# Zero-padded full-height score matmuls in a two-layer hybrid attention backbone

## The reference

```python
def _diff_attn(q, k, v, lam):
    s = jnp.einsum('bqhid,bkhid->bhiqk', q, k, preferred_element_type=jnp.float32)
    p = jax.nn.softmax(s * (ATTN_HEAD_DIM ** -0.5), axis=-1)
    a = p[:, :, 0] - lam * p[:, :, 1]
    return jnp.einsum('bhqk,bkhe->bqhe', a.astype(v.dtype), v)
```

## Time and profile before

| | |
|---|---|
| median of 3 runs | 1786.41 us (1783.9 to 1787.53) |
| profiled execution: time | 1787.53 us |
| profiled execution: span from first to last instruction | 1785.6 us |
| busy: TensorE, VectorE, ScalarE, GpSimd | 1716.1, 1084.9, 609.5, 76.4 us |
| mean granted clock of TensorE | 0.984 |
| attention, layer 0 | 557 to 602 us |
| attention, layer 1 | 1524 to 1553 us |

### The profile page before, as it was taken

One profiled execution on the slowest core, in us unless ns is written; L12 is line 12 of the kernel. 1 busy time (PEld: TensorE's weight loads), 2 busy tenths in 40 slices (PEclk: granted clock), 3 DMA queues, 4 the chain that ended last, 5 costly groups with the idle time before them and its releaser, 6 DMA issues.

```text
span 1785.6 us, 25611 instructions
## 1 busy us (share of the span) xinstructions
PE 1716.1 (96%) x8952; PEld 1446.0 (81%) x8952; DVE 1084.9 (61%) x1666; ACT 609.5 (34%) x905; POOL 76.4 (4%) x140
## 2 busy tenths in 40 slices
PE   3999999999998999999999999999999999799999
PEld 1888888887785678888888878888888878589999
DVE  2877777235678667777762377777523277665544
ACT  2322222124534643222221242222222263544443
POOL 0000000000001000000000000000000000000000
PEclk9999999999999999999999999999999999899999
DMA  9355555332241125555552225555333224035554
GB/s 362 130 187 177 176 178 175 106 95 71 91 134 48 36 71 177 177 176 177 175 177 94 95 83 189 176 178 183 109 96 104 84 85 149 28 130 180 185 179 151
DMA packets 69684, 248.62 MB, mean 139 GB/s; under 512 B 7424, under 2 KB 8448, under 8 KB 69504
## 3 DMA queue, kind: packets, MB, share of 16 engines
q1 hardware_dynamic: 51200, 180.79, 31.3%
q0 software_dynamic: 18432, 67.12, 11.6%
HBM read 246.83 MB, written 1.05 MB: 139 GB/s over the span
## 4 chain that ended last, share of the span: by engine, by line
PE 90%; DVE 5%; ACT 2%; SPq 1%; issue 1%; DMA 1%; DVEq 0%; ACTq 0%
PE ps L973 28%; PE ps L975 28%; PE ps L974 28%; PE ps L1025 3%; DMA raw<-wstream 1%; DVE shared_b L683 1%; DVE wlo L582 1%; DVE nmax L871 1%; PE ps L1191 1%; PE ps L1164 1%; DVE xl L669 1%; SPq L270 1%; ACT prob L484 1%; PE ps L1112 0%; SPq L266 0%
## 5 line engine op out<-in xcount | busy, mean ns | idle before, releaser
L582 DVE TENSOR_TENSOR wlo<-raw,whi 128x1024 fp32r<-128x1024 f32 x320 | 392.1, 1225 | 603.5 <-ACT whi L330 602.8
L973 PE MATMUL ps<-xh,whi 128*128 128x512 f32 (+1 forms) x1880 | 683.0, 363 | 23.1 <-DVE xl L669 18.3
L330 ACT ACTIVATE whi<-raw 128x1024 fp32r<-128x1024 f32 x320 | 339.1, 1060 | 1064.3 <-PE ps L975 1047.6
L975 PE MATMUL ps<-xh,wlo 128*128 128x512 f32 (+1 forms) x1880 | 665.2, 354 | 0.0
L974 PE MATMUL ps<-xl,whi 128*128 128x512 f32 (+1 forms) x1880 | 665.0, 354 | 0.0
L973 PEld LDWEIGHTS ps<-xh,whi 128*128 128x128 f32 x1880 | 361.3, 192 | 81.3 <-issue 25.3
L974 PEld LDWEIGHTS ps<-xl,whi 128*128 128x128 f32 x1880 | 362.9, 193 | 49.3 <-issue 3.8
L975 PEld LDWEIGHTS ps<-xh,wlo 128*128 128x128 f32 x1880 | 362.3, 193 | 47.8
L604 DVE SCALAR_TENSOR_TENSOR shared_a<-wm,cs,shared_a 128x512 f32<-128x512 f32 x448 | 307.6, 747 | 0.0
L973 PE MATMUL ps<-ah,whi 128*128 (+2 forms) x704 | 255.5, 363 | 0.0
L975 PE MATMUL ps<-ah,wlo 128*128 (+2 forms) x704 | 255.2, 363 | 0.0
(11 more groups left out here) (101 smaller groups left out, 842.1 us busy)
## 6 DMA issues: line engine op xcount, KB each, us to landing
raw<-wstream SPq DMA_DIRECT2D x320, 512.0 KB, 3.4
wm<-wmod POOLq DMA_DIRECT2D x128, 512.0 KB, 3.6
wm<-wmod SPq DMA_DIRECT2D x3, 2048.0 KB, 21.8
h<-x_t SPq DMA_DIRECT2D x1, 2048.0 KB, 12.7
wm<-wmod SPq DMA_DIRECT2D x2, 1024.0 KB, 20.7
K<-cols SPq DMA_DIRECT2D x1, 1163.0 KB, 14.4
out_t<-h SPq DMA_DIRECT2D x8, 128.0 KB, 2.5
K<-cols SPq DMA_DIRECT2D x1, 269.0 KB, 2.8
```

Of the source, the lines that this page charges most:

```text
L330: act.activation(whi[:, n % SPL, :, :].rearrange("p a b -> p (a b)"), raw[:, s, :], ACT.Copy)\
L582: dve.tensor_tensor(wlo[:, n % SPL, :, :].rearrange("p a b -> p (a b)"), raw[:, n % RAW, :], whi[:, n % SPL, :, :].rearrange("p a b -> p ( ...
L973: pe.matmul(out_ap, hi_w, hi_x, start=start, stop=False)
L975: return pe.matmul(out_ap, lo_w, hi_x, start=False, stop=stop)
```

## The change

The scores' two half-height matmuls become two full-height ones. The key chunk is used whole as the moving side. The stationary side is a query chunk in which the other half is zero: for the first product `kq`'s own chunk, whose partitions 64 to 127 are cleared after being copied away; for the second a chunk of `cx` (2, 3, 6, 7 for the four heads), whose partitions 64 to 127 receive that copy and whose partitions 0 to 63 are cleared. ScalarE makes the copy after the second value block's split, GpSimd clears the `cx` halves once the pool is done, VectorE clears the `kq` halves after the pool's scaling and before its next split. TensorE waits for both clears in place of `qk_ready`. The tile `qws` shrinks from 16 to 2 columns.

```diff
+        Z = (2, 3, 6, 7)
...
+            def query_zeros(l):
+
+                pool.wait_ge(pooled_done, 2 * (l + 1))
+                for a in range(2):
+                    ins = pool.memset(cx[0:DH, Z[2 * a]:Z[2 * a] + 2, 0:ntile(l)], 0.0)
+                ins.then_inc(q_zero, 1)
...
             loads(u0 // 2 + 1, after_mix)
+            query_zeros(0)
             conv_pool_low(0)
             loads(after_mix, UNITS * PAIRS // 2)
+            query_zeros(1)
             conv_pool_low(1)
...
                 for b in range(VB - 1):
                     split_next(n0 + CV + b)
+                    if b == 1:
+
+                        act.wait_ge(pooled_done, 2 * (l + 1))
+                        act.wait_ge(qk_ready, 8 * (l + 1))
+                        for a in range(2):
+                            ins = act.activation(cx[DH:P, Z[2 * a]:Z[2 * a] + 2, 0:w],
+                                                 kq[DH:P, H + 2 * a:H + 2 * a + 2, 0:w], ACT.Copy)
+                        ins.then_inc(q_copied, 1)
...
+                        dve.wait_ge(q_copied, l + 1)
+                        dve.memset(kq[DH:P, H:2 * H, 0:w], 0.0).then_inc(q_ready, 1)
                         split_next(n0 + b)
...
-                pe.wait_ge(qk_ready, 8 * (l + 1))
+                pe.wait_ge(q_ready, l + 1)
+                pe.wait_ge(q_zero, l + 1)
                 pe.wait_ge(y_done, Y0[l] + 4)
...
-                    for b in range(2):
-                        rows = slice(DH * b, DH * b + DH)
-                        ins = pe.matmul(ps[:, 2 * (u % 2) + b, 0:wk], kq[rows, H + hd, t * P:(t + 1) * P],
-                                        kq[rows, hd, a:a + wk], start=True, stop=True)
+                    for b, q in enumerate((kq[:, H + hd, :], cx[:, Z[hd], :])):
+                        ins = pe.matmul(ps[:, 2 * (u % 2) + b, 0:wk], q[:, t * P:(t + 1) * P],
+                                        kq[:, hd, a:a + wk], start=True, stop=True)
                     ins.then_inc(score_done, 1)
```

More of the change, by code:

```diff
@@ L106, in program @@
         lamc = sb("lamc", [P, DEPTH, 8])
-        qws = sb("qws", [P, 16])
+        qws = sb("qws", [P, DEPTH])
         lamt = sb("lamt", [P, 2, DH])
@@ L197, in program @@
         qk_ready = sem("qk_ready")
+        q_copied = sem("q_copied")
+        q_zero = sem("q_zero")
+        q_ready = sem("q_ready")
         score_done = sem("score_done")
@@ L819, in lambda_sums @@
                 dve.sem_inc(lam_red, 1)
-                own(dve.tensor_scalar(qws[:, 0:DEPTH], col("qw", 0, DEPTH), DH ** -0.5, None, ALU.mult))
+                own(dve.tensor_scalar(qws[:, :], col("qw", 0, DEPTH), DH ** -0.5, None, ALU.mult))
             def lambda_ends():
```

## The result

| | before | after |
|---|---|---|
| median | 1786.41 us (1783.9 to 1788.88, 5 runs) | 1797.49 us (1795.21 to 1800.09, 5 runs) |
| ratio after/before, 95% interval | | 1.0068, 1.0055 to 1.0082 |
| profiled execution: time, span | 1787.53, 1785.6 us | 1795.21, 1794.2 us |
| mean granted clock | 0.984 | 0.991 |

The kernel became slower by 12 us (0.0068 x 1786.4; the medians differ by 11.1), four times the forecast's +2.8 and outside its range. The page of the kernel after hardly shows it: span, busy time by engine, and the shares of the chain that ended last, which answer to the earlier trace rows.

A forecast was written before the change was run, and what follows sets the result against it. Matmuls bound the kernel (TensorE 90% of the span); in attention three engines' limits lie within 0.2 us. Layer 1's 1.9 + layer 0's 1.2 - 0.3 at entries = +2.8 on 1786.4: 1789.2 us, range 1785.5 to 1794.

The forecast's parts named there:

- the forecast's +2.8: Whole kernel: both layers' attention costs 1.9 + 1.2 - 0.3 = +2.8 us, giving 1789.2 us; chance 0.64.
- Removed is nothing else; the smaller qws tile costs nothing: End of the preparation's costing: nothing else is removed, and shrinking the tile qws costs nothing.
- A score costs 0.86 instead of half of it: TensorE, attention scores: full-height matmuls lack the halves' overlap, +0.86 us per 512-key unit, +0.43 per 256-key unit, loads hidden.
- Layer 1: +1.9, less 0.15 at the entry: Layer 1's attention: eighth maximum +1.9 us later, passed through whole to the layer's end, less 0.15 at entry.
- Layer 0: +1.2, less 0.15: Layer 0's attention: eighth maximum +1.1 us, with short units (0.06 each at most) +1.2, less 0.15 at entry.
- the walk: Attention followed unit by unit, each engine in its order; layer 0's eighth maximum at 580.2 against 579.02.
- The clock is kept in attention: Both attentions: shorter TensorE pauses (1.3, 1.1 and 1.2 us) keep the granted clock at 1.00 in the first 14 us.
- The preparation, costed at nothing: Before the first scores: copies and clears hide beside the last value blocks, cover 2.7 us (VectorE) and 2.5 us (GpSimd).
- The clock fell: Rival: the clock falls in attention all the same; one layer +4.8 us, both +6.8 (1791.2 to 1793.2); chance 0.23.
- preparation was not late: Rival: late clears delay layer 0's first scores, each microsecond counting once, 5 us late giving 1794; chance 0.04.
- The rival that priced two of these stretches at 6.4 us: Slow-clock stretches at 1560 (3.4 us) and from 658 (3.0 us) both spared, giving 1782.8 us; chance 0.08.

## Why the prediction was wrong

- **"Removed is nothing else; the smaller qws tile costs nothing"** is the step that failed. The edit removed 56 bytes, and with them the alignment of `ah` and `al`. It was costed as an instruction would be, and it has none. Measured: +8.8 us when done alone, 9.3 when undone, 3.4 us in the stretch of one FFN. The rest of the sum came out: with the tile left at 16 columns the kernel takes 1789.43 us, where the forecast said 1789.2. That the two lie 0.2 us apart is luck: the interval is 1.3 to 4.5 us for the forecast's +2.8, and the term of layer 0 was set too low.
- **A score costs 0.86 instead of half of it.** Right. Four full-height steps take 1.73 us in the chain of the kernel after (4 x 0.43), and the two queries' loads add nothing between them. The Trainium skill, TensorE: Matmul & The Clock Gate, under "What overlaps and what doesn't", would have had it otherwise: by it a weight load overlaps running matmuls only when the row groups differ. The trace does not agree, since four instructions with loads of full height stand 0.43 us apart, no further than in the earlier trace rows.
- **Layer 1: +1.9, less 0.15 at the entry.** From the first scores (1523.98, 1532.36) to the last low part (1560.24, 1570.36) 36.26 us became 38.00: +1.7. Right.
- **Layer 0: +1.2, less 0.15.** Too low. From first scores to last low part 55.92 us became 58.40: +2.5, over twice the forecast. The eighth maximum came 24.0 us after the first scores (582.45 - 558.49), before 22.1; the walk had 23.2. So 0.8 was lost in the long units and the rest in the short ones, which it gave almost nothing. One pair of executions measures this only roughly: the kernels with the scores of the kernel before and no fills take 55.9 to 57.3 us here, and the kernel after with `qws` of 16 columns takes 59.9, so the layer costs 1.1 us more at the least. The two layers' sum of 4.2 lies within the interval of the timed 2.8 (1.3 to 4.5).
- **The clock is kept in attention.** Right, 1.00 for the first 14 us of both. The pauses became 1.08 and 0.63 us where 1.3 and 1.1 were worked out. The two runs that differ from it show the cause: half-height scores bring the fall back, half-height scores twice as long take it away. One reading was off. Two pauses, of 1.95 and 1.49 us, are said to lie before the fall in layer 1, but the clock is at 0.50 from 1529.24 on the earlier trace rows and the second pause began at 1529.04 (it ended at 1530.53), so only the first lies before it. And in layer 0 the kernel after kept its clock over a pause of 1.72 us (570.57 to 572.29), so no length of pause can be given as the limit.
- **The preparation, costed at nothing.** Right: ScalarE's copies 2.0 us (2.1 forecast), VectorE's clear 1.8 (1.8), GpSimd's 1.8 (1 to 5.3), and with half-height scores behind it a ratio of 1.0000.
- **Rivals.** None of them held it. The clock fell in neither layer, preparation was not late, and the slow stretches beyond attention became shorter in the profiled execution (434 to 440: 0.72) but did not go. Stretches just as short stand in traces of kernels that time as the one before, so this can't be put down to the change. The rival that priced two of these stretches at 6.4 us set them high, if fills in every pause are the measure: they won 2.7 us net of their own time.

The prediction's list of edits was complete; its question to each was which engine does more or less work. For a tile declaration the question is what moves.

## To carry to other kernels

When a tile's size changes, work out the start addresses of the tiles behind it, and compare a matmul-only stretch far from the edit between the two traces before explaining a difference by the edit's own instructions. In a kernel whose chain is 90% matmul, 3% on the step of one loop outweighed all that was done to attention; keep the start of a streamed operand where its steps were measured fastest for its number of columns, with a named gap rather than by chance. A pause of TensorE that lets the clock fall can be filled with matmuls nobody reads, and here it paid only when the pauses behind the norms and before the output projection were filled as well.

## What the runs showed of the hardware

- The step of a 512-column matmul that streams from SBUF depends on the start address of the streamed operand, counted from the program's first tile: 0.2267 us at a multiple of 128 bytes, 0.2289 at 64 beyond one, 0.2333 at 32 on either side of one, 0.2367 with `ah` at 4 and `al` at 68 beyond, when both operands of the triple are off. The f32 scores (0.43 us an instruction) showed nothing. Matmuls of 256 columns went the other way: 120.3 ns a step at a multiple of 128, 118.3 to 118.8 at 32 or 64 off, 121.5 at 4 and 68. The Trainium skill, SBUF — State Buffer, under "Operand start alignment", lets an fp32 operand start at any multiple of its 4 bytes and says that this is about legality and not speed; the runs agree that such starts work, and add a price.
- One moved operand among three matmuls costs 70% of the price of all three (2.37 of 3.37 us), not one third; the steps into it and behind its neighbour lengthen too (231.4 and 228.6 ns, its own 234.3, from 226.7).
- In attention the clock fell behind a pause of 1.95 us and stayed up behind pauses of 1.08 and 0.63 us, but also behind one of 1.72; behind one of 2.12 us it fell in one kernel and stayed up in another. Longer half-height matmuls kept it as well as full-height ones.
